# Two sister kernels' RG-LRU and norm edits joined in a two-block transformer, with MLA, dilated and neighbourhood reorderings

## The chip, the cores and the metric

The kernel runs on one core of a Trainium2 chip. The metric is the device time of one execution in microseconds, 3506.21 as the median of three runs (3505.55 to 3506.93). TensorE multiplies, VectorE, ScalarE and GpSimd do the elementwise work, SyncE issues the transfers. In the profile they are PE, DVE, ACT, POOL and SP, and PEld is TensorE's loading of stationary operands.

## What is computed

All data is float32, one sequence of 512 tokens with 1024 channels. The first block has two layers with three mixers side by side, gated, an output projection and a SwiGLU. The second has retention, a SwiGLU, an RG-LRU and a SwiGLU, each between two norms.

```python
def first_block(x, ...):
    for l in range(DEPTH):                                   # 2
        h = rms_norm(x, g_mix[l])
        c_q, c_kv, k_r, qkv_b, qkv_c, gate_logits = jnp.split(h @ w_in[l], IN_SPLITS, axis=-1)
        y_a = mla_mixer(c_q, c_kv, k_r, ...)                 # 8 heads, 512 x 512 scores
        y_b = dilated_mixer(q_b, k_b, v_b)                   # 3 patterns, banded
        y_c = neighbourhood_mixer(q_c, k_c, v_c, rpb[l])     # 8 heads, windows on a grid
        gates = jax.nn.sigmoid(gate_logits)
        x = x + (gates[0] * (y_a @ w_pa[l]) + gates[1] * (y_b @ w_pb[l]) + gates[2] * (y_c @ w_pc[l])) @ w_o[l]
        h = rms_norm(x, g_ffn[l])
        x = x + (jax.nn.silu(h @ w1[l]) * (h @ w3[l])) @ w2[l]
    return rms_norm(x, g_final)

def rglru_mixer(x, ...):
    y_branch, u = jnp.split(x @ w_in, 2, axis=-1)            # 1536 channels each
    y_branch = jax.nn.gelu(y_branch, approximate=True)
    u = conv4(u) + conv_b                                    # causal, per channel
    r, i = jax.nn.sigmoid(blocked(u, gate_w) + gate_b)       # 6 blocks of 256
    log_a = -8.0 * r * jax.nn.softplus(-a_param)
    a, mult = jnp.exp(log_a), jnp.sqrt(-jnp.expm1(2.0 * log_a))
    h = scan(a, mult * i * u)                                # h[t] = a[t] * h[t-1] + b[t]
    return (h * y_branch) @ w_out

def second_block(x, ...):
    for layer in range(DEPTH):
        m = retention_mixer(rms_norm(x), ...) if layer == 0 else rglru_mixer(rms_norm(x), ...)
        x = x + rms_norm(m, norm_g[layer, 1])
        x = x + rms_norm(swiglu_ffn(rms_norm(x, norm_g[layer, 2]), ...), norm_g[layer, 3])
```

## The kernel before

Activations lie with channels on the partitions and the 512 tokens along the free axis. Each float32 product is three TensorE passes: an operand is split into a high part and the rest (names in h and l: `zh` and `zl`, `u_ush` and `u_usl`, `u_hyh` and `u_hyl`), and high x high, low x high and high x low are added in a PSUM bank. Weights come in chunks of eight 128 x 128 tiles: SP's queue brings `raw`, ScalarE copies `wh` (line 525), VectorE subtracts `wl` (line 552), with a ring of three. The order of each engine is written by hand, one function for an engine and a stage (`tensor_`, `scalar_`, `vector_`, `gpsimd_`), and each engine runs in order. `wait_ge` is a wait on an event that another engine's `tell` announces; `claim(b, ...)` makes TensorE wait until the former contents of PSUM bank b have been read. The splits of the next chunks stand in ScalarE's and VectorE's programs where `ahead` or `reach(mark, n)` puts them: `reach` splits up to the n-th chunk behind a mark.

MLA (`tensor_mla`) runs 32 units of scores, with the transposes of probabilities `m_p` (by `ident`) three units later and the values, into bank 7, six later. Between the units TensorE takes tiles of the dilated projections from `rest`, eight to a group in bank 0, which ScalarE's `scalar_b` copies to `b_qk`, and query tiles from `q`. `scalar_y_move` and `vector_y_add` empty the values' bank into `m_yf`.

The dilated stage (`scalar_dil`, `vector_dil`) and the neighbourhood (`tensor_nbr`, `scalar_nbr`, `vector_nbr`, `gpsimd_nbr`) are iterations of the same kind. In the latter one iteration has two score tiles of 128 x 256; GpSimd divides `c_p` by its sum, and TensorE transposes the tiles of the iteration before.

A norm stage (`tensor_post`, named `ret`, `f20`, `f21`, `lru` in the tables `POST_BANK`, `POST_AT`) runs the last output tile `m7` in two halves of 256 tokens, takes the mean square by one-column matmuls with `ones`, spreads the root over the partitions (`hrows`), adds the result to `x`, and makes `z` for the next projection. For that projection's norm a tree (`TREE`) adds the eight squares `mb` on GpSimd and VectorE, and four one-column matmuls sum the rest (`tensor_next_stat`).

RG-LRU (`tensor_lru`, `scalar_lru`, `vector_lru`, `gpsimd_lru`) runs six blocks b of two channel tiles. TensorE: `gates(b)`, then the `u` and `y` projections of block b + 2, and the output's first pairs behind block 4. VectorE: scan of b - 1, conv of the next tiles in four steps (`vector_conv`, `u_uc`), their low part, `y_in` (which empties the y banks into `u_y`), low part of `hy`, then the recurrence: `vector_recur_in` (`iu`, and the relu `t`), `vector_recur` (`d`, `w`, `aa`). ScalarE does tanh, exp, square root and gelu's tanh, GpSimd the `+1` on `u_t`, gelu's products on `u_q` and the products with `u_g`. One buffer of a tile, `G[2]`, holds `t`, then the scan, then `hv`, until `hy` is read.

## Time and profile before

| what | us |
|---|---|
| median of 3 runs | 3506.21 |
| profiled execution | 3503.95 |
| its span | 3502.2 |
| TensorE busy | 3375.8 |
| VectorE busy | 1833.2 |
| ScalarE busy | 1285.5 |
| GpSimd busy | 626.8 |
| stretches: MLA of layer 0 / neighbourhood of layer 0 | 93.5 / 124.0 |
| norm after retention / after the first SwiGLU / after RG-LRU | 42.2 / 38.8 / 42.0 |
| RG-LRU | 265.6 |

The mean granted clock of TensorE is 0.983 of full speed. The rows further down are read so: a stretch's length beside the busy time of an engine tells how much of it the engine stood; a granted clock under 1.00 tells that part of the stretch ran at the lower of two levels (1.2 instead of 2.4 GHz); a wait is listed with the engine and tile that ended it.

### The profile page before, as it was taken

Reading aid. Unit: us, or ns where it says so; the run is one execution under the profiler, and the core shown is the slowest. Engines: PE = TensorE matmul, PEld = TensorE weight load, DVE = VectorE, ACT = ScalarE, POOL = GpSimd, SP = SyncE. Lnnn points to the kernel's source line nnn. Section 1 sums busy time; section 2 is a strip of 40 time slices with the busy share of each in tenths; the row PEclk is TensorE's granted clock in tenths of the full one; section 3 lists DMA queues with packets and bytes.
Section 4 is the critical chain, followed back from the end, with each engine's and each line's share of the span. In section 5 each row is a group of like instructions: output and inputs, shape, how many; then the busy total and the mean of one; then the engine's idle time right before and its main releaser. Section 6 shows DMA issues by size and latency. Waiting matters only on the chain.

```text
span 3502.2 us, 38259 instructions
## 1 busy us (share of the span) xinstructions
PE 3375.8 (96%) x15476; PEld 2788.2 (80%) x15476; DVE 1833.2 (52%) x2720; ACT 1285.5 (37%) x1958; POOL 626.8 (18%) x572
## 2 busy tenths in 40 slices
PE   8899999999999999999999999999999988889998
PEld 7787778888888877778888878888888876678887
DVE  6755565544437564655444455544444359855433
ACT  4643453322226433543332323333232235533221
POOL 1420122011003210221110022112110025431101
PEclk9999999999999999999999999999999999889999
DMA  3012223222221121223223222221323222222322
GB/s 131 31 61 73 74 89 99 97 96 98 99 93 55 49 73 64 89 83 102 91 96 105 98 75 82 88 90 67 102 97 97 84 67 76 75 72 97 96 96 85
DMA packets 85425, 296.91 MB, mean 85 GB/s; under 512 B 9472, under 2 KB 11776, under 8 KB 85248
## 3 DMA queue, kind: packets, MB, share of 16 engines
q1 hardware_dynamic: 85248, 294.47, 25.2%
q8 instruction: 122, 2.00, 0.2%
q14 instruction: 55, 0.45, 0.0%
HBM read 292.33 MB, written 2.10 MB: 84 GB/s over the span
## 4 chain that ended last, share of the span: by engine, by line
PE 83%; DVE 8%; ACT 4%; POOL 2%; issue 2%; DMA 0%; SPq 0%; POOLq 0%; DVEq 0%; ACTq 0%
PE bank L308 81%; PE bank L311 2%; DVE wl L552 2%; ACT wh L525 1%; POOL x L572 1%; DVE u_t L548 1%; POOL mb L572 1%; DVE u_uc L548 1%; DVE small L1198 1%; ACT c_k L525 1%; ACT u_g L528 0%; DVE u_t L545 0%; DVE m_ptl L552 0%; ACT b_v L525 0%; DVE c_kf L542 0%
## 5 line engine op out<-in xcount | busy, mean ns | idle before, releaser
L552 DVE TENSOR_TENSOR wl<-raw,wh 128x1024 fp32r<-128x1024 f32 (+1 forms) x532 | 681.1, 1283 | 902.6 <-ACT wh L525 899.7
L308 PE MATMUL bank<-zh,wh 128*128 128x512 f32 (+1 forms) x2668 | 1044.3, 391 | 20.6 <-ACT zh L525 7.8
L308 PE MATMUL bank<-zh,wl 128*128 128x512 f32 (+1 forms) x2668 | 1035.6, 388 | 14.3 <-DVE wl L552 14.3
L308 PE MATMUL bank<-zl,wh 128*128 128x512 f32 (+1 forms) x2668 | 1035.0, 388 | 14.2 <-DVE zl L555 14.0
L525 ACT ACTIVATE wh<-raw 128x1024 fp32r<-128x1024 f32 (+1 forms) x532 | 557.8, 1052 | 600.5 <-PE bank L308 499.9
L308 PEld LDWEIGHTS bank<-zh,wh 128*128 128x128 f32 x2668 | 509.4, 191 | 126.0 <-ACT zh L525 7.8
L308 PEld LDWEIGHTS bank<-zh,wl 128*128 128x128 f32 x2668 | 509.3, 191 | 122.0 <-DVE wl L552 20.2
L308 PEld LDWEIGHTS bank<-zl,wh 128*128 128x128 f32 x2668 | 509.3, 191 | 111.5 <-DVE zl L555 16.4
L308 PE MATMUL bank<-f_mh,wh 128*128 128x512 f32 (+1 forms) x748 | 285.0, 381 | 0.0
L308 PE MATMUL bank<-f_mh,wl 128*128 128x512 f32 (+1 forms) x748 | 283.0, 378 | 0.0
L308 PE MATMUL bank<-f_ml,wh 128*128 128x512 f32 (+1 forms) x748 | 282.1, 377 | 0.0
L572 POOL TENSOR_TENSOR f_t<-f_t 128x512 f32<-128x512 f32 x88 | 113.4, 1289 | 791.6 <-DVE f_t L548 791.6
L578 POOL TENSOR_TENSOR small<-small 128x1 f32<-128x1 f32 (+3 forms) x35 | 45.0, 1285 | 961.1 <-DVE small L545 961.1
L308 PEld LDWEIGHTS bank<-f_mh,wl 128*128 128x128 f32 x748 | 140.5, 188 | 28.9 <-DVE wl L552 0.4
L308 PE MATMUL bank<-wh,zh 128*128 128x512 f32 (+1 forms) x384 | 154.0, 401 | 8.7 <-ACT wh L525 4.1
L308 PEld LDWEIGHTS bank<-f_ml,wh 128*128 128x128 f32 x748 | 140.6, 188 | 26.8
L308 PEld LDWEIGHTS bank<-f_mh,wh 128*128 128x128 f32 x748 | 140.9, 188 | 25.6
L528 ACT ACTIVATE f_t<-f_t 128x512 f32<-128x512 f32 x88 | 55.6, 632 | 270.1 <-DVE f_t L542 270.0
L308 PE MATMUL bank<-wl,zh 128*128 128x512 f32 (+1 forms) x384 | 152.8, 398 | 0.5 <-DVE wl L552 0.5
L308 PE MATMUL bank<-wh,zl 128*128 128x512 f32 (+1 forms) x384 | 152.4, 397 | 0.0
L525 ACT ACTIVATE f_mh<-f_t 128x512 fp32r<-128x512 f32 x88 | 55.6, 632 | 227.2 <-POOL f_t L572 227.2
L542 DVE TENSOR_TENSOR f_t<-bank,rrow 128x512 f32<-128x512 f32 x88 | 60.7, 689 | 121.3 <-PE bank L308 110.7
(340 smaller groups left out, 4645.4 us busy)
## 6 DMA issues: line engine op xcount, KB each, us to landing
raw<-in_wts SPq DMA_DIRECT2D x530, 512.0 KB, 3.3
c_nb<-in_c_bias SPq DMA_DIRECT2D x16, 384.0 KB, 3.2
x<-in_xT SPq DMA_DIRECT2D x8, 256.0 KB, 6.6
out<-x SPq DMA_DIRECT2D x16, 128.0 KB, 1.9
b_mask<-in_b_mask SPq DMA_DIRECT2D x2, 576.0 KB, 3.7
r_d<-in_decay SPq DMA_DIRECT2D x4, 256.0 KB, 2.7
raw<-in_wts SPq DMA_DIRECT2D x2, 256.0 KB, 3.5
m_t<-in_mla_tab SPq DMA_DIRECT2D x2, 256.0 KB, 4.9
```

Source lines behind the costliest of these rows:

```text
L308: return self.e.matmul(out, l, r, start=start, stop=stop, skip_group_check=inside)
L311: return self.e.transpose(out, in_, self.m.ident)
L525: return self.e.activation(out, in_, ACT.Copy, scale=scale)
L528: return self.e.activation(out, in_, func, **kw)
L542: return self.e.tensor_tensor(out, a, b, op)
L548: return self.e.scalar_tensor_tensor(out, a, s, b, op0, op1)
L552: return self.e.tensor_tensor(out, src, b32(hi), ALU.subtract)
L572: return self.e.tensor_tensor(out, a, b, op)
L578: return self.e.tensor_tensor(out, v, self.m.negh[:, 0:n], ALU.pow)
L1198: L.e.tensor_reduce(m.mn[:, c:c + 1], m.bank[4 + i % 2], AX.X, ALU.min).then_inc(*L.tell("mn", "mla", l, i))
```

## The change

RG-LRU: conv step 0, relu, `+1`, `aa` and gelu's square term (times a constant, plus another) become ScalarE activations; the scan writes its own buffers `u_h`; the factor -0.125 moves from `hy` into the norm (`POST_SCALE`); the loops of ScalarE and VectorE and the splits among them (`LRU_REACH`) are put in another order; the tail's output pairs are cut into other chunks. Norms: the tree goes, and TensorE sums each square on its own, after each k of the second half's pass and in the next group. MLA: the values alternate between banks 1 and 7 (the last in 4), and the fill tiles are spread by a table over eight units. Neighbourhood: transposes, division and values move by one iteration. Dilated: the fill slots, and where the copy stands.

```diff
--- before.py
+++ after.py
...
+def values_bank(key, h):
+
+    if key[0] != "mla":
+        return 7
+    return {6: 7, 7: 4}.get(h, (1, 7)[h % 2])
...
-V_BANK = (4, 5, 0, 1)
+V_BANK = (5, 0, 1, 3)
...
-        next(rest, None)
+        for _ in range((0, 1, 1, 1, 2, 1, 1, 1)[i % 8] if i else 1):
+            next(rest, None)
...
-SLOTS = {0: [5] * 8 + [4] * 2, 1: [8] * 2 + [7] * 8}
+SLOTS = {0: [6] + [5] * 7 + [4, 3], 1: [8] * 2 + [7] * 8}
...
+        for n in () if p else at(p, i, 1):
+            scalar_b(L, ("b", l, 1) + n)
...
-    for it in range(18):
-        if 1 <= it < 17:
-            ps = L.claim(6, "lo", "pt", *key, it - 1)
-            for u in (2 * it - 2, 2 * it - 1):
+    for it in range(19):
+        if 2 <= it < 18:
+            j = it - 2
+            ps = L.claim(6, "lo", "pt", *key, j)
...
-        if it >= 3 and it % 2:
-            h = (it - 3) // 2
+        if it >= 4 and it % 2 == 0:
+            h = (it - 4) // 2
...
-            j = it - 1
+    for it in range(21):
+        if it >= 5 and it % 2 and it < 20:
+            scalar_y_move(L, m.b_yt, (it - 5) // 2, *key)
+        if 2 <= it < 18:
+            j = it - 2
...
         if 1 <= it < 17:
-            j = it - 1
+            for i in (2 * it - 2, 2 * it - 1):
+                vector_div(L, i, *key)
...
+POST_SCALE = {"ret": 1.0, "f20": 1.0, "f21": 1.0, "lru": -0.125}
+POST_AT = {"ret": 0, "f20": 3, "f21": 3, "lru": 0}
+POST_ROWS = {"ret": 7, "f20": 9, "f21": 9, "lru": 7}
...
-             [[("ev", "m7", s, h)] for h in range(2)], {(1, 2): squares, (1, 6): rows}, False)
+             [[("ev", "m7", s, h)] for h in range(2)], {(1, 2): squares, (1, POST_ROWS[s]): rows}, False)
...
-            if h == 0 and n == POST_AT[s]:
+            if h == 0 and n == POST_AT[s] + 1:
                 vector_m7(L, s, g, 1)
-            if h == 0 and n == max(POST_AT[s] + 1, 3):
+            if h == 0 and n == POST_AT[s] + 2:
+                if nxt:
+                    L.reach(("z2", s), 1)
                 stat(1)
-            if h or n > 1:
+            if nxt and h == 0 and n == POST_AT[s] + 4:
+                L.reach(("z2", s), 2)
+            if h:
...
-        for n, d in TREE[3:]:
-            L.wait_ge(*tree_ready(s, n, d, 1)[0])
-            L.wait_ge(*tree_ready(s, n, d, 1)[1])
-            L.tt(half(m.mb[n], 1), half(m.mb[n], 1), half(m.mb[n - d], 1), ALU.add).then_inc(
-                *L.tell("sq", "tree", s, n, d, 1))
...
-    def squares():
-        ps = L.claim(6, "rv", *N)
-        L.wait_ge("pl", "tree", s, 7, 4, 0)
-        L.wait_ge("sq", "tree", s, 7, 4, 1)
-        L.sums(ps, False, 0, m.mb[7], True).then_inc(*L.tell("st", "stat", *N))
-
-    return squares, L.spread(N)
+    def squares(h, ns):
+        def go():
+            ps = L.claim(6, "rv", *N) if (h, ns[0]) == (0, 0) else m.bank[6]
+            for n in ns:
+                L.wait_ge("cp", "xsq", s, n, h)
+                for r in (2 * h, 2 * h + 1):
+                    new = (h, n, r) == (0, 0, 0)
+                    t = L.mm(ps[:, r:r + 1], m.mb[n][:, 128 * r:128 * r + 128], m.ones, new, new or n == 7, not new)
+            if (h, ns[-1]) == (1, 7):
+                t.then_inc(*L.tell("st", "stat", *N))
+        return go
+
+    return ({(1, k): squares(0, (k,)) for k in range(8)}, {k: squares(1, (2 * k, 2 * k + 1)) for k in range(4)}, L.spread(N))
...
-             {(0, 1): squares1, (0, 3): rows1})
-    squares, rows = tensor_next_stat(L, prev)
+             {(0, 0): squares1, (0, 3): rows1, **early})
...
-            tensor_post_pair(L, "lru", 0, LW, x, lru_out_desc, range(8))
-    for i in (2, 4):
-        tensor_post_pair(L, "lru", i, LW, x, lru_out_desc, range(8))
+            for i in (0, 2):
+                tensor_post_pair(L, "lru", i, LW, x, lru_out_desc, range(8))
+    tensor_post_pair(L, "lru", 4, LW, x, lru_out_desc, range(8))
+    tensor_post_pair(L, "lru", 6, LW, x, lru_out_desc, range(10))
     for i in (0, 2, 4):
-        tensor_post_pair(L, "lru", i, LW, x, lru_out_desc, range(8, LW))
-    tensor_post(L, "lru", LW, x, lru_out_desc, 6)
+        tensor_post_pair(L, "lru", i, LW, x, lru_out_desc, range(8, 10))
+    for i in (0, 2, 4, 6):
+        tensor_post_pair(L, "lru", i, LW, x, lru_out_desc, range(10, LW))
+    tensor_post(L, "lru", LW, x, lru_out_desc, 8)
...
+def scalar_conv(L, n):
+
+    m = L.m
+    L.wait_ge("ev", "u", n)
+    if n > 3:
+        L.wait_ge("ev", "iu", n - 4)
+        L.wait_ge("lo", "us", n - 4)
+    L.fn(m.u_uc[n % 4], m.u_pad[n % 2][:, 0:512], ACT.Identity, scale=m.col("conv0")[:, n:n + 1],
+         bias=m.col("conv_b")[:, n:n + 1]).then_inc(*L.tell("cp", "conv", n))
...
+    L.wait_ge("cp", "y2", n)
+    L.fn(q, q, ACT.Identity, scale=0.044715 * 0.7978845608028654, bias=m.gel).then_inc(*L.tell("cp", "y3", n))
...
-            L.wait_ge("lo", "hy", j - 2)
+            L.wait_ge("ev", "d", j - 2)
+            L.wait_ge("th", "s", j - 2)
         L.fn(G[2], G[0], ACT.Tanh, scale=C, bias=C).then_inc(*L.tell("th", "t", j))
     for i in range(2):
         j = 2 * b + i
         G, C = recur_bufs(m, b, i), m.sp4[:, j:j + 1]
+        if b:
+            L.wait_ge("pl", "k", j - 2)
+            L.wait_ge("cp", "aa", j - 2)
         L.fn(G[3], G[0], ACT.Exp, scale=C, bias=C).then_inc(*L.tell("ex", "x", j))
+    for i in range(2):
+        j = 2 * b + i
+        G = recur_bufs(m, b, i)
+        L.wait_ge("th", "t", j)
+        L.fn(G[2], G[2], ACT.Relu).then_inc(*L.tell("cp", "t", j))
+        L.wait_ge("ex", "x", j)
+        L.fn(G[3], G[3], ACT.Identity, bias=m.ones).then_inc(*L.tell("cp", "v", j))
...
-        L.ts(G[2], G[2], 0.0, 1.0, ALU.max, ALU.mult).then_inc(*L.tell("ev", "t", j))
...
+def scalar_recur_a(L, b):
+    for i in range(2):
+        j = 2 * b + i
+        G = recur_bufs(L.m, b, i)
         L.wait_ge("ev", "w", j)
-        L.ts(G[4], G[3], -0.5, -1.0, ALU.mult, ALU.add).then_inc(*L.tell("ev", "aa", j))
+        L.fn(G[4], G[3], ACT.Identity, scale=-0.5, bias=L.m.neg1).then_inc(*L.tell("cp", "aa", j))
...
-        L.e.tensor_tensor_scan(G[2], G[4], G[0], 0.0, ALU.mult, ALU.add).then_inc(*L.tell("ev", "scan", j))
+        L.e.tensor_tensor_scan(L.m.u_h[i], G[4], G[0], 0.0, ALU.mult, ALU.add).then_inc(*L.tell("ev", "scan", j))
...
-LRU_REACH = {b: (2, 2, 3, 3, 4, 4) if b == 4 else (2, 3, 3, 4, 5, 6) for b in range(6)}
+LRU_REACH = (3, 3, 4, 5, 5, 6)
...
         lru_reach(L, b, 0)
-        for n in nxt:
-            scalar_us(L, n)
+        if b < 6:
+            scalar_recur(L, b)
         lru_reach(L, b, 1)
         if b:
             scalar_hy(L, b - 1)
+        for n in nxt:
+            scalar_us(L, n)
         lru_reach(L, b, 2)
-        if b < 6:
-            scalar_recur(L, b)
-        lru_reach(L, b, 3)
         for n in nxt:
             scalar_y_square(L, n)
+        lru_reach(L, b, 3)
         if b < 6:
             scalar_recur_sqrt(L, b)
+            scalar_recur_a(L, b)
...
         lru_reach(L, b, 0)
         if nxt:
             vector_conv(L, nxt)
+        lru_reach(L, b, 1)
+        if b:
+            vector_hy(L, b - 1)
         for n in nxt:
             vector_us(L, n)
-        lru_reach(L, b, 1)
         for n in nxt:
             vector_y_in(L, n)
-        if b:
-            vector_hy(L, b - 1)
+        if b < 6:
+            vector_recur_in(L, b)
         lru_reach(L, b, 2)
         if b < 6:
-            vector_recur_in(L, b)
+            vector_recur(L, b)
         lru_reach(L, b, 3)
-        if b < 6:
-            vector_recur(L, b)
-        lru_reach(L, b, 4)
         if b < 4:
             for n in (2 * b + 4, 2 * b + 5):
                 vector_pad(L, n)
+        lru_reach(L, b, 4)
         for n in nxt:
             vector_gelu(L, n)
...
```

VectorE in RG-LRU, from the scan of one block to the next; `u_t` is the recurrence, `u_uc` the conv, `u_g` the gates. Before:

```order
L3052 SCALAR_TENSOR_TENSOR u_t<-u_t,u_g 128x512 x2
L552 TENSOR_TENSOR wl<-raw,wh 128x1024
L545 TENSOR_SCALAR u_uc<-u_pad,cols 128x512 x2
L548 SCALAR_TENSOR_TENSOR u_uc<-u_pad,cols,u_uc 128x512 x6
L552 TENSOR_TENSOR u_usl<-u_uc,u_ush 128x512 x2
L552 TENSOR_TENSOR wl<-raw,wh 128x1024
L542 TENSOR_TENSOR u_y<-bank,rrow 128x512 x2
L555 SCALAR_TENSOR_TENSOR u_hyl<-u_t,u_hyh 128x512 x2
L548 SCALAR_TENSOR_TENSOR u_g<-u_g,u_uc 128x512 x2
L545 TENSOR_SCALAR u_t<-u_t 128x512 x2
```

After:

```order
L3076 SCALAR_TENSOR_TENSOR u_h<-u_t,u_g 128x512 x2
L553 TENSOR_TENSOR wl<-raw,wh 128x1024 x2
L549 SCALAR_TENSOR_TENSOR u_uc<-u_pad,cols,u_uc 128x512 x6
L553 TENSOR_TENSOR u_hyl<-u_h,u_hyh 128x512 x2
L553 TENSOR_TENSOR u_usl<-u_uc,u_ush 128x512 x2
L543 TENSOR_TENSOR u_y<-bank,rrow 128x512 x2
L549 SCALAR_TENSOR_TENSOR u_g<-u_g,u_uc 128x512 x2
L553 TENSOR_TENSOR wl<-raw,wh 128x1024
L549 SCALAR_TENSOR_TENSOR u_t<-u_t 128x512 x4
L553 TENSOR_TENSOR wl<-raw,wh 128x1024
L543 TENSOR_TENSOR u_pad<-bank,rrow 128x512 x2
```

The tensor-scalar steps are gone, `u_hyl` stands ahead of `u_usl` and `u_y`, two chunks are split behind the scan, and the last split before the recurrence `u_t` ... x4 is as it was.

ScalarE in the same block, from the gates' tanh (`u_g<-bank`) to the splits behind. Before:

```order
L528 ACTIVATE u_g<-bank,cols 128x512 x4
L525 ACTIVATE wh<-raw 128x1024
L525 ACTIVATE u_ush<-u_uc 128x512 x2
L525 ACTIVATE wh<-raw 128x1024
L525 ACTIVATE u_hyh<-u_t 128x512 x2
L528 ACTIVATE u_t<-u_g,cols 128x512 x2
L528 ACTIVATE u_t<-u_g,small 128x512 x2
L525 ACTIVATE wh<-raw 128x1024
L528 ACTIVATE u_q<-u_y 128x512 x2
L528 ACT_TABLE_LOAD
L528 ACTIVATE u_g<-u_t 128x512 x2
L525 ACTIVATE wh<-raw 128x1024
```

After:

```order
L529 ACTIVATE u_uc<-u_pad,cols 128x512 x2
L529 ACTIVATE u_g<-bank,cols 128x512 x4
L526 ACTIVATE wh<-raw 128x1024 x2
L529 ACTIVATE u_t<-u_g,cols 128x512 x2
L529 ACTIVATE u_t<-u_g,small 128x512 x2
L529 ACTIVATE u_t<-u_t 128x512
L529 ACTIVATE u_t<-u_t,small 128x512
L529 ACTIVATE u_t<-u_t 128x512
L529 ACTIVATE u_t<-u_t,small 128x512
L526 ACTIVATE u_hyh<-u_h 128x512 x2
L526 ACTIVATE u_ush<-u_uc 128x512 x2
L526 ACTIVATE wh<-raw 128x1024
```

The recurrence, with four further steps, now stands ahead of `u_hyh` and `u_ush`, and the conv's first step ahead of the gates.

TensorE in MLA's units 7 and 8 (`m_pth`, `m_ptl` with `m_v` are values, `zh`, `zl` with `wh1`, `wl1` fill tiles of bank 0, `m_zqh0` queries). Before:

```order
L308 MATMUL bank7<-m_ptl1,m_v 128x256
L308 MATMUL bank7<-m_pth1,m_v 128x256
L308 MATMUL bank7<-m_ptl1,m_v 128x256
L308 MATMUL bank0<-zh,wh1 128x512 [waits cp]
L308 MATMUL bank0<-zl,wh1 128x512
L308 MATMUL bank0<-zh,wl1 128x512
L311 MATMUL bank6<-ident,m_p2 128x128 [waits sc,lo]
L311 MATMUL bank6<-ident,m_p2 128x128 x3
L308 MATMUL bank5<-m_kah,m_qh0 128x512 [waits ex]
L308 MATMUL bank5<-m_kal,m_qh0 128x512
L308 MATMUL bank5<-m_kah,m_ql0 128x512
```

After:

```order
L309 MATMUL bank5<-m_kbh,m_qh1 128x512 [waits ex]
L309 MATMUL bank5<-m_kbl,m_qh1 128x512
L309 MATMUL bank5<-m_kbh,m_ql1 128x512
L309 MATMUL bank2<-m_zqh0,wh1 128x512 [waits ev]
L309 MATMUL bank2<-m_zql0,wh1 128x512
L309 MATMUL bank2<-m_zqh0,wl1 128x512
L309 MATMUL bank0<-zh,wh1 128x512 [waits cp]
L309 MATMUL bank0<-zl,wh1 128x512
L309 MATMUL bank0<-zh,wl1 128x512
L312 MATMUL bank3<-ident,m_p1 128x128 [waits sc,lo]
L312 MATMUL bank3<-ident,m_p1 128x128 x3
```

The fill tile that opens a new group, the one that waits for `cp`, stands behind the queries of unit 7 instead of the values of unit 8.

## Rows read from the trace of the kernel before

**Rows 1.** The page, part 1: busy us (share of span) xinstructions by engine
```profile
PE 3375.8 (96%) x15476; PEld 2788.2 (80%) x15476; DVE 1833.2 (52%) x2720; ACT 1285.5 (37%) x1958; POOL 626.8 (18%) x572
```

**Rows 2.** By stretch: length, busy PE PEld DVE ACT POOL, clock, DMA share, GB/s
```profile
414.00:538.00 124.00, 117.25 (x531) 90.70 (x530) 84.36 (x176) 63.96 (x129) 31.90 (x45) 0.97 0.24 79
2420.10:2462.30 42.20, 31.95 (x188) 29.23 (x187) 23.32 (x43) 16.78 (x34) 21.94 (x25) 0.80 0.16 51
2803.00:2841.80 38.80, 31.61 (x187) 29.15 (x186) 23.31 (x44) 15.84 (x32) 20.34 (x24) 0.82 0.21 69
3107.40:3149.40 42.00, 31.48 (x187) 29.04 (x187) 24.07 (x44) 17.59 (x36) 22.66 (x26) 0.80 0.15 51
```

**Rows 3.** Waits of TensorE, whole run: total us, times, longest
```profile
PE bank L308 <- DVE wl L552: 36.4, 17, 4.7
PE bank L308 <- DVE m_yf L542: 10.2, 8, 1.7
PE bank L311 <- POOL c_p L575: 8.9, 9, 2.0
PE bank L308 <- ACT b_qk L525: 6.4, 4, 1.9
PE bank L311 <- POOL b_p L575: 1.7, 2, 0.9
```

**Rows 4.** By stretch, RG-LRU: blocks one and three, and the tail
```profile
2878.20:2909.70 31.50, 27.91 (x122) 22.38 (x121) 29.47 (x33) 17.61 (x24) 13.90 (x11) 1.00 0.23 73
2946.60:2982.00 35.40, 30.06 (x123) 23.73 (x122) 30.44 (x35) 18.95 (x27) 15.88 (x13) 0.95 0.24 75
3018.00:3107.40 89.40, 79.87 (x359) 65.62 (x357) 67.38 (x74) 40.14 (x56) 29.37 (x22) 0.92 0.23 77
```

**Rows 5.** By tile, VectorE, 2878.2 to 3018: ns min/median/max, first, last start
```profile
L545 DVE TENSOR_SCALAR u_t<-u_t x16: 415/1161/1517, 2892.0 to 3006.2; 128x512 f32<-128x512 f32 x16
L552 DVE TENSOR_TENSOR wl<-raw,wh x20: 1214/1226/2309, 2879.9 to 3012.2; 128x1024 fp32r<-128x1024 f32 x20
L545 DVE TENSOR_SCALAR u_uc<-u_pad,cols x8: 535/543/543, 2881.1 to 2985.0; 128x512 f32<-128x512 f32 x8
```

**Rows 6.** Timeline, VectorE, third block: start, us, operation
```profile
2972.52 2.28 DVE L552 TENSOR_TENSOR wl<-raw,wh 128x1024 fp32r<-128x1024 f32 x1
```

**Rows 7.** Timeline, TensorE, same place; in brackets idle before and releaser
```profile
2974.85 0.80 PE L308 MATMUL bank<-u_ush,wl 128*128 128x512 f32 x1 [4.71 <-DVE wl L552]
```

**Rows 8.** Groups by shape, ScalarE, 2878.2 to 3018: busy us, mean ns, idle
```profile
L528 ACT ACTIVATE u_t<-u_g,cols 128x512 f32<-128x512 f32 x8 | 6.1, 807 | 6.3 <-DVE u_hyl L555 6.3
L528 ACT ACTIVATE u_q<-u_y 128x512 f32<-128x512 f32 x8 | 4.5, 614 | 0.0
```

**Rows 9.** Groups by shape, GpSimd, 2878.2 to 3018: busy us, mean ns, idle
```profile
L575 POOL TENSOR_SCALAR u_q<-u_q 128x512 f32<-128x512 f32 x8 | 8.5, 1069 | 3.4 <-ACT u_q L528 3.1
```

**Rows 10.** Waits of TensorE, 2419.5 to 2462.3, norm after retention
```profile
PE bank L308 <- DVE zl L555: 6.3, 3, 3.0
PE bank L308 <- DVE wl L552: 3.9, 1, 3.9
```

**Rows 11.** Timeline, TensorE: column sums, and the matmul behind them
```profile
2459.91 0.95 PE L308 MATMUL bank<-small,mb 128*128 128x1 f32 x8
2460.72 0.48 PE L308 MATMUL bank<-zh,wh 128*128 128x512 f32 x1
```

**Rows 12.** By tile, GpSimd, 2420 to 2465: ns min/median/max, first, last start
```profile
L572 POOL TENSOR_TENSOR mb<-mb x10: 722/771/924, 2443.4 to 2450.9; 128x256 f32<-128x256 f32 x10
```

**Rows 13.** Timeline, TensorE, MLA of the first layer, behind unit 7's queries
```profile
95.26 0.40 PE L308 MATMUL bank<-zh,wh 128*128 128x512 f32 x1
95.49 0.39 PE L308 MATMUL bank<-zl,wh 128*128 128x512 f32 x1
```

**Rows 14.** Timeline, ScalarE, same place: exp of unit 7, the copy
```profile
95.47 0.69 ACT L528 ACTIVATE m_p<-bank,small 128x512 f32<-128x512 f32 x1
96.16 0.60 ACT L525 ACTIVATE b_qk<-bank 128x512 f32<-128x512 f32 x1
```

More of the change, by code:

```diff
@@ L296, in block2 @@
         self.u_q = [T(f"u_q{i}", 52.25 + i) for i in range(2)]
+        self.u_h = [T(f"u_h{i}", 54.25 + i) for i in range(2)]
 class Pe(Line):
@@ L1161, in scalar_mla @@
     L.lead = 0
-    for i in range(40):
+    for i in range(41):
         if i and i % 8 == 0 and i <= 32:
@@ L1223, in gpsimd_mla @@
     m = L.m
-    for i in range(40):
+    for i in range(41):
         if 1 <= i < 33:
@@ L1489, in scalar_dil @@
             scalar_exp(L, i, m.b_p[i % 2], m.b_p[i % 2], *key)
+        for n in at(p, i, 1) if p else ():
+            if n[0] == "g":
+                scalar_gate(L, l, 0, n[1])
         if i in (5, 9):
@@ L1544, in vector_dil @@
                 *L.tell("mn", *key, i, 1))
+        for x, n in at(p, i, 1) if p else ():
+            if x == "g":
+                vector_gate(L, l, 0, n)
+            else:
+                vector_proj(L, l, 0, n)
         if 1 <= i < 9:
@@ L1774, in vector_nbr @@
     L.lead = 0
-    for it in range(20):
+    for it in range(21):
         if it < 16:
@@ L1805, in vector_nbr @@
                 (vector_gate if x == "g" else vector_proj)(L, l, 1, n)
+        if it >= 8 and it % 4 == 0:
+            vector_y(L, m.b_yf, *m.yc, (it - 8) // 4, (it - 8) // 4, *key)
+        for x, n in at_n(it, 2):
+            if x in "qk":
+                (vector_c_q_lo if x == "q" else vector_c_k_lo)(L, l, n)
         L.ahead()
@@ L1819, in gpsimd_nbr @@
     gpsimd_bias(L, l, 1)
-    for it in range(20):
-        if it < 16:
-            for i in (2 * it, 2 * it + 1):
+    for it in range(21):
+        if 1 <= it < 17:
+            for i in (2 * it - 2, 2 * it - 1):
                 gpsimd_div(L, i, L.m.c_p[i % 6], *key)
@@ L2598, in scalar_m7 @@
     L.wait_ge("mm", "acc", "m", s, 7, h)
-    L.fn(half(m.rrow, h), half(m.bank[POST_BANK[s][7 + h]], h), ACT.Square).then_inc(*L.tell("cp", "m7", s, h))
+    L.fn(half(m.rrow, h), half(m.bank[POST_BANK[s][7 + h]], h), ACT.Square,
+         scale=POST_SCALE[s]).then_inc(*L.tell("cp", "m7", s, h))
 def vector_m7(L, s, g, h):
@@ L2624, in scalar_post @@
             L.wait_ge("sq", "m", s, n - 1)
-        L.fn(m.sqt if n else m.sqa, m.bank[POST_BANK[s][n]], ACT.Square).then_inc(*L.tell("cp", "msq", s, n))
+        L.fn(m.sqt if n else m.sqa, m.bank[POST_BANK[s][n]], ACT.Square, scale=POST_SCALE[s]).then_inc(
+            *L.tell("cp", "msq", s, n))
     scalar_m7(L, s, 0)
@@ L2772, in tensor_ffn2 @@
         L.group(n, 8, L.z_whole(), f2_in_desc, [f_bank(i, w) for w in range(2)], [("ev",) + x for x in n],
-                {2: rows} if i == 2 else {})
+                {1: rows} if i == 2 else {})
     x = mids_of(L, F)
@@ L3097, in scalar_lru @@
     scalar_rows(L, ("z2", "f20"), False)
+    for n in range(2):
+        scalar_conv(L, n)
     for n in range(2):
@@ L3107, in scalar_lru @@
         nxt = (2 * b + 2, 2 * b + 3) if b < 5 else ()
+        for n in nxt:
+            scalar_conv(L, n)
         if b < 6:
```

154 lines of the change are left out of this document (56 added, 98 removed).

## The prediction

> **What bounds the kernel now.** I read the page first: TensorE is busy for 3375.8 of 3502.2 us [rows 1]. So there are two ways to gain, an idle TensorE and a TensorE at the lower clock, and the next views look for both. The table by stretch gives the places: the three output-norm stages (42.2, 38.8 and 42.0 us) and the neighbourhood (124.0 us) are places in which TensorE is neither full nor at clock 1.00 [rows 2], and so are the RG-LRU's blocks and tail [rows 4]. The list of TensorE's waits names the causes over the whole run: 36.4 us for a low weight half (`wl`), 10.2 us for the MLA values' bank (`m_yf`), 8.9 us for neighbourhood probabilities (`c_p`), 6.4 us for `b_qk`, 1.7 us for `b_p` [rows 3]. All of them stand on VectorE, ScalarE or GpSimd, in-order engines that had something else ahead.
>
> Every sum is made against the profiled execution, 3503.95 us; the median shown, 3506.21, lies 2.26 us above, and I add that at the end. About 0.2% (7 us) is what a measurement of this kernel can tell from no change.
>
> **RG-LRU, the four blocks between gates 0 and gates 4.** They take 2878.2 to 3018.0, 139.8 us, 31.5 for the first and 35.4 for the third [rows 4]. TensorE needs 27.9 us for a block, its busy time in the first, at clock 1.00 [rows 4]. VectorE sets the pace: two tensor-scalar steps on each `u_t` (relu and `aa`, 16 in four blocks) take 415 to 1517 ns, the low weight half 1214 ns, but up to 2309 [rows 5]. In the third block one takes 2.28 us, and starts behind those [rows 6]; TensorE stands 4.71 us for it and then falls to the lower clock, which the block's 0.95 holds [rows 4, 7].
>
> The change takes from VectorE, per block, 2 conv steps of 0.54, 2 relus of at least 0.42 and 2 `aa` of up to 1.52: 4 us or so of 30.4 [rows 4, 5]. GpSimd loses two `+1` and two gelu steps of 1.07 [rows 9]. ScalarE gains ten operations: two with two pointers of 0.81, the others like the square of 0.61: 2 x 0.81 + 8 x 0.61 = 6.5 us, on an engine that the third block keeps waiting (18.95 busy of 35.4) [rows 4, 8]. The new order puts `wl` ahead of `y_in`, and the scan writes a buffer of its own, so that the tanh of the next block no longer waits for `hy`.
>
> What is late next? `y_in` now stands behind `hy` and `us`, and these stand behind ScalarE's longer recurrence: TensorE's next y pair claims the bank that `y_in` empties. From a walk through the new order with these durations I find TensorE stopped there about 1.5 us a block, which gives 29.4; a stretched operation more or less makes it 28.2 to 31.0. I take 29.6, since the wait adds up behind in-order engines: 4 x 29.6 = 118.4, **-21 us** (-16 to -27).
>
> A rule speaks against this part. The Trainium skill (Perfetto Trace Analysis, "Optimizing Scalar/DVE Operations") says that an operation for which VectorE has a fast mode is quicker there and that moving it pays if VectorE is saturated. By the page's average it isn't (52%), and the six steps would cost ScalarE more than they free; the sum by that would be 0 for this term. In this stretch VectorE is busy 30.44 of 35.40 us, so I take the stage.
>
> **RG-LRU, start and tail.** The start (conv 0 on ScalarE, rows of `z` earlier) gives **-2** (0 to -4). From gates 4 to the end of the output's sixth pair it is 89.4 us with TensorE busy 79.9 at clock 0.92 [rows 4]: 9.5 us idle and, at 8% of the clock, 7.2 lost. The new order puts four output chunks ahead of gates 5, which covers most of that idle time, not the wait for the last `hy`: **-10** (-5 to -15).
>
> **Output norms (three stages, 123.0 us).** Their clock is 0.80 to 0.82 [rows 2]. In the first TensorE waits 6.3 us for `zl` and 3.9 for `wl` [rows 10]. The latter is held by the adds of the tree, ten of 722 to 924 ns on GpSimd and four on VectorE, which VectorE's split of the next chunk stands behind [rows 12]; the tree goes. In its place TensorE sums the columns: eight one-column matmuls are 0.81 us for four of the program's [rows 11], 28 more a stage are 5.7 us, 17.0 in all. Eight of them a stage stand in the second pass, where TensorE waits for `zl` anyway; the later ones have no cover. So: gaps and clock loss over the three stages are 28 idle and 24 of clock (20% of 42.2, 18% of 38.8, 20% of 42.0); 17 comes on; what goes is 11 of `wl` wait, the clock loss behind it (some 8), and some 9 of `zl` from sums and splits that come earlier. -28 + 17 = **-11** (+6 if only the `wl` wait goes, -19).
>
> **Neighbourhood (twice).** The transposes wait for GpSimd's division of the same iteration, 8.9 us over both layers [rows 3], and the clock of 0.97 over 124 us is 3.7 more [rows 2]. One iteration later the division is done. Next is `c_kl`, whose low half VectorE makes after the gates now; I leave about 1.5 us a layer: **-8** (-3 to -12).
>
> **MLA (twice).** Two banks for the values take off most of the 10.2 us for `m_yf`, but where it waits 1.7 the chain of `q` on VectorE is next, so I count 5, and 3 of `b_qk` and of the first values. Against that stands a wait the change adds: fill tiles move within the eight units, and the ninth, 17th and 25th open a new group in bank 0 one unit earlier, before ScalarE has copied the old. In the profile TensorE is behind the queries of unit 7 at 95.26 and goes on with the eighth tile; after the change the ninth stands there. ScalarE's exp of unit 7 starts at 95.47 and the copy that it would wait for comes behind it, 96.16 + 0.60 [rows 13, 14]. That is 1.5 us, six times: +9. Queued behind it on TensorE are the transposes and the scores of the next unit. Net **+1** (-6 to +7).
>
> **Dilated and tail.** Of `b_p` (1.7) and what is left of `b_qk` I count **-3** (0 to -5) [rows 3]. In the last norm the rows come nine 256-column matmuls later, at half the 0.23 us between two 512-column ones [rows 13] about 1 us, with cover for half: **+0.5** (0 to +1).
>
> Sum: -21 - 2 - 10 - 11 - 8 + 1 - 3 + 0.5 = **-53.5**: 3450.5 profiled, **3452.7** median.
>
> **Rivals.** (a) More goes than I count. If VectorE's and GpSimd's operations stretch each other (0.415 against 1.517, 1.214 against 2.309 [rows 5]) and six fewer a block ends it, the blocks come to 28, the tail to 75, and the norm stages to 104: -28 - 3 - 15 - 19 with -11 for the neighbourhood, -5 for the dilated stage and -3 for MLA is -84, or 3422. The Trainium skill (SBUF — State Buffer, "Who interferes with whom") has it as a lock: the later of the two waits the other out, and ScalarE never waits; the rows' stretch of about 1.1 us is what it would look like. For it: the steps' median of 1.161 us lies nearer the long end. Against: the scan, conv and GpSimd's large adds stay. (b) The sums on TensorE aren't covered: norm stages +6 instead of -11, 3470. For it: the last half of the sums stands in a group with nothing to wait for. (c) The recurrence on ScalarE makes a longer chain, blocks at 32.5 (130 in all, -10), tail -4, the others near their weak bounds (norms -8, neighbourhood -5, MLA +3, dilated -2): -26, 3480; with blocks at 38 (152, +12) it is -4, no difference. (d) Slower: ScalarE as the new limit. `aa` now stands behind the square root, which loads a table, and the scan, `hv`, `hy`, `us` and `y_in` stand behind `aa`, in this order on two engines. If each handover is late the loop slips by a chain, not by an engine. The other terms are -20.5 without the LRU; five blocks have to rise by over 4.1 us, from 35.0 to 39.1, for the kernel to be slower. At 42: 5 x 7 - 20.5 = +14.5, 3521. Against it: ScalarE's 18.95 + 6.5 is 25.5 of 35.4. That the change doesn't do what it says is out for the moved instructions, which stand in the new order; a wait that only moves to the next event is in (c).
>
> **How the numbers follow.** The forecast has 0.44 (3438 to 3465), (a) 0.16, (b) 0.13, (c) 0.18, of which 0.05 are within 0.2%, (d) 0.09. Faster by over 0.2%: 0.44 + 0.16 + 0.13 + 0.13 = 0.86; same 0.05; slower 0.09. The range goes from 3422, (a), to 3490, (c) without its part close to zero; 0.18 lie outside.
>
> **What would show it.** LRU blocks of 29 to 30 us between gates, no `wl` wait over 1 us there, and waits for `u_y` of 1 to 2 us. In the norms no `wl` wait of 3 to 4 us, one-column matmuls of 0.2 us each, and stages of 37 to 40. In MLA waits for `b_qk` of about 1.5 us three times a layer, none for `m_yf` over 1. In the neighbourhood no `c_p` wait over 0.5. I am wrong if a block takes over 32 us, or if the norm stages don't shrink.

## The result, and the profile after

The changed kernel takes 3467.82 us (median of four runs, 3462.23 to 3471.03) against 3505.99, the kernel before measured alongside, a ratio of 0.9889 with a 95% interval of 0.9872 to 0.9906: 38 us faster. The forecast was 3452.7, with a range of 3422 to 3490. The size is 15 us short: two terms of the sum are wrong by 20 us together, in the same direction, and others came out a little better.

The span went from 3502.2 to 3466.1 us. The table sets the stages of the two traces side by side, each from the end of one named group of matmuls to the end of another. The first row runs from the last tile of MLA's value projection to the neighbourhood's first score group, in both layers; MLA's own row ends a little inside the dilated stage, so it is longer than the 93.5 us a layer of the table ahead.

| stage | before | after | change | forecast |
|---|---|---|---|---|
| MLA and dilated, twice | 676.4 | 689.7 | +13.3 | -2 |
| of these MLA | 270.8 | 284.8 | +14.0 | +1 |
| neighbourhood, twice | 256.0 | 255.0 | -1.0 | -8 |
| three norm stages | 123.0 | 111.4 | -11.7 | -11 |
| RG-LRU, start to gates 0 | 36.4 | 33.9 | -2.6 | -2 |
| gates 0 to gates 4 | 139.7 | 115.1 | -24.7 | -21 |
| RG-LRU's tail | 89.4 | 81.0 | -8.4 | -10 |
| all else | | | -1.0 | +0.5 |

The page of the changed kernel (busy us, share of the span, instructions) has the answer to [rows 1]. TensorE is busy as long as before, in a span 36 us shorter:

```profile
PE 3376.0 (97%) x15644; PEld 2796.1 (81%) x15644; DVE 1796.0 (52%) x2674; ACT 1321.6 (38%) x2018; POOL 600.6 (17%) x518
```

TensorE's waits in the changed kernel, whole run (total us, times, longest), beside [rows 3]:

```profile
PE bank L309 <- ACT b_qk L526: 16.2, 8, 3.1
PE bank L309 <- DVE c_kl L553: 10.4, 4, 3.8
...
PE bank L309 <- DVE m_kal L553: 8.0, 4, 2.3
...
PE bank L309 <- DVE u_y L543: 4.9, 3, 1.8
...
PE bank L309 <- DVE wl L553: 1.2, 2, 0.7
...
PE bank L309 <- DVE m_yf L543: 0.9, 2, 0.6
```

Of 36.4 us for `wl` 1.2 are left, of 10.2 for `m_yf` 0.9, and `c_p` is gone. But `b_qk` rose from 6.4 to 16.2, and two names are new with more than a few us: `c_kl` (0.9 before) and `m_kal`. That is where most of the missing time is: beside the forecast 13 us are missing in MLA, 7 in the neighbourhood and 2 in the dilated stage.

The stretches of the changed kernel (length, busy PE PEld DVE ACT POOL, clock, DMA) that answer to [rows 2, 4], the norms first, then RG-LRU's second and fourth block and its tail:

```profile
2432.67:2470.46 37.79, 33.30 (x243) 31.70 (x243) 21.02 (x39) 17.37 (x36) 13.83 (x15) 0.95 0.18 60
2810.96:2847.77 36.81, 34.56 (x244) 33.30 (x244) 19.64 (x36) 16.21 (x33) 11.82 (x13) 0.91 0.23 75
...
2908.90:2937.90 29.00, 27.71 (x122) 22.52 (x121) 26.26 (x29) 24.99 (x37) 17.16 (x8) 1.00 0.29 99
...
2967.30:2996.70 29.40, 27.62 (x121) 22.42 (x120) 27.30 (x30) 24.98 (x36) 18.50 (x8) 1.00 0.26 90
2996.70:3077.70 81.00, 76.67 (x359) 64.31 (x358) 59.00 (x67) 48.36 (x70) 35.37 (x18) 0.96 0.26 87
3077.70:3114.50 36.80, 34.31 (x244) 32.61 (x243) 21.07 (x39) 17.36 (x36) 13.86 (x15) 0.91 0.19 61
```

A block takes 29.4 us with TensorE busy 27.6 at full clock, where the third took 35.4 at 0.95. The norms have a clock of 0.91 to 0.95 instead of 0.80 to 0.82.

Now the new waits, each with what stands in front. In MLA, TensorE (timeline; start, us, in brackets idle before and what ended it) behind the queries of unit 7, and ScalarE in front of that, the place of [rows 13, 14]:

```profile
98.53 0.50 PE L309 MATMUL bank<-zh,wh 128*128 128x512 f32 x1 [2.33 <-ACT b_qk L526]
```

```profile
96.27 0.69 ACT L529 ACTIVATE m_p<-bank,small 128x512 f32<-128x512 f32 x1 [0.65 <-DVE small L1209]
...
96.94 1.04 ACT L526 ACTIVATE wh<-raw 128x1024 fp32r<-128x1024 f32 x1
97.89 0.58 ACT L526 ACTIVATE b_qk<-bank 128x512 f32<-128x512 f32 x1
```

The wait forecast is there, at the forecast place, behind exp of unit 7. A weight split of 1.04 us stands between exp and copy as well. This is so at the first of the six forecast waits only. Four of them are 1.3 to 1.5 us, and in the longest, 3.15 us in the first layer, no split stands there: exp itself starts late, since the maximum that it waits for stands behind a split on VectorE. TensorE, ScalarE and VectorE there:

```profile
152.56 0.79 PE L309 MATMUL bank<-zh,wh 128*128 128x512 f32 x1 [3.15 <-ACT b_qk L526]
```

```profile
151.25 0.69 ACT L529 ACTIVATE m_p<-bank,small 128x512 f32<-128x512 f32 x1 [1.66 <-DVE small L1209]
```

```profile
149.14 1.47 DVE L553 TENSOR_TENSOR wl<-raw,wh 128x1024 fp32r<-128x1024 f32 x1 [1.65 <-ACT wh L526]
```

Some 20 us after the first of these waits, TensorE stands before values in bank 1, and VectorE (below it) has been making the low part of keys from that same bank, behind the addition that empties the values' other bank:

```profile
118.97 0.39 PE L309 MATMUL bank<-m_pth,m_v 128*128 128x256 f32 x1 [1.75 <-DVE m_kal L553]
```

```profile
116.81 0.67 DVE L553 TENSOR_TENSOR m_ptl<-bank,m_pth 128x512 fp32r<-128x512 f32 x1
117.52 0.68 DVE L543 TENSOR_TENSOR m_yf<-bank,m_yt 64x512 f32<-64x512 f32 x1
118.23 0.68 DVE L553 TENSOR_TENSOR m_kal<-bank,m_kah 64x512 fp32r<-64x512 f32 x1
```

The neighbourhood, TensorE before scores of the third head pair, and VectorE ahead of it:

```profile
473.94 0.58 PE L309 MATMUL bank<-c_k,c_q 128*128 128x256 f32 x1 [3.78 <-DVE c_kl L553]
```

```profile
469.22 0.68 DVE L543 TENSOR_TENSOR f_g<-bank,rrow 128x512 f32<-128x512 f32 x1
470.66 0.69 DVE L549 SCALAR_TENSOR_TENSOR f_g<-f_g,bank 128x512 f32<-128x512 f32 x1 [0.77 <-ACT f_g L529]
471.27 2.62 DVE L553 TENSOR_TENSOR c_kl<-c_kf,c_k 64x640 fp32r<-64x640 f32 x2
```

The low keys stand behind a gate and its projection, which itself waited 0.77 us for ScalarE.

### The profile page after: what moved, and what is told of

Read it like the earlier page. It is cut to its first block, busy times and chain, and to the rows that moved or that the text cites. A ratio compares the mean times of both kernels' runs of the same rounds, so it can differ in the third digit from the quotient of the medians.

```text
span 3466.1 us, 38536 instructions
## 1 busy us (share of the span) xinstructions
PE 3376.0 (97%) x15644; PEld 2796.1 (81%) x15644; DVE 1796.0 (52%) x2674; ACT 1321.6 (38%) x2018; POOL 600.6 (17%) x518
## 3 DMA queue, kind: packets, MB, share of 16 engines
q1 hardware_dynamic: 85248, 294.47, 25.5%
## 4 chain that ended last, share of the span: by engine, by line
PE 89%; DVE 6%; ACT 3%; issue 1%; POOL 1%; DMA 0%; SPq 0%; POOLq 0%; DVEq 0%; ACTq 0%
PE bank L309 87%; PE bank L312 2%; DVE wl L553 1%; ACT wh L526 1%; DVE small L1209 1%; DVE u_uc L549 1%; DVE m_ptl L553 0%; ACT u_g L529 0%; ACT b_v L526 0%; ACT m_p L529 0%; ACT c_k L526 0%; POOL x L573 0%; DVE m_yf L543 0%; DVE c_kl L553 0%; POOL u_g L573 0%
## 5 line engine op out<-in xcount | busy, mean ns | idle before, releaser
L309 PE MATMUL bank<-zh,wh 128*128 128x512 f32 (+1 forms) x2668 | 1043.5, 391 | 30.0 <-ACT b_qk L526 11.1
L543 DVE TENSOR_TENSOR f_t<-bank,rrow 128x512 f32<-128x512 f32 x88 | 60.7, 689 | 123.3 <-PE bank L309 112.6
## 6 DMA issues: line engine op xcount, KB each, us to landing
x<-in_xT SPq DMA_DIRECT2D x8, 256.0 KB, 6.5
r_d<-in_decay SPq DMA_DIRECT2D x4, 256.0 KB, 2.7
raw<-in_wts SPq DMA_DIRECT2D x2, 256.0 KB, 3.4
m_t<-in_mla_tab SPq DMA_DIRECT2D x2, 256.0 KB, 4.9
```

Source lines behind the costliest of these rows:

```text
L309: return self.e.matmul(out, l, r, start=start, stop=stop, skip_group_check=inside)
L543: return self.e.tensor_tensor(out, a, b, op)
```

## Experiments

Each kernel is the changed kernel with the edit shown (the last two join edits); times are medians of four runs and compare with 3467.82. Stage lengths are taken as in the table, from one trace each. The kernel before was measured beside every group of runs, with medians of 3503.2 to 3506.0, so a difference of 2 or 3 us between kernels of different groups says nothing. Stages vary too, where the code of the stage is the same: MLA as changed takes 281.0 to 286.8 us in eight traces, the neighbourhood as changed 252.8 to 255.0 in nine (253.9 on the mean; the changed kernel's own is the longest), the three norm stages 109.5 to 112.4, RG-LRU 228.6 to 231.4.

**MLA.** Three kernels separate fill order and value banks. All of MLA back, which also splits the values one unit earlier again:

```diff
-V_BANK = (5, 0, 1, 3)
+V_BANK = (4, 5, 0, 1)
...
-    return {6: 7, 7: 4}.get(h, (1, 7)[h % 2])
+    return 7
...
-        for _ in range((0, 1, 1, 1, 2, 1, 1, 1)[i % 8] if i else 1):
-            next(rest, None)
+        next(rest, None)
```

> The changed kernel with MLA's value banks (all in bank 7), fill order (one tile a unit) and value split put back as they were before. Own theory: MLA as changed costs 16 us net (7 in the first layer, 9 in the second, by the ends of the stages in the two traces), nothing behind it depends on it, so this kernel is 16 us faster than the changed one, about 3452, with b_qk waits of 6 instead of 16 us and none for m_kal; m_yf waits of 10 come back. Rival A: the loss only stands in MLA because the dilated stage behind took it back (that stage gained 5.6 where 3 were expected), so 16 - 5 = 10 or less comes, about 3458. Rival B: what was lost in MLA is a clock or other accident of that run: no difference, 3468.

It took 3450.29 us (ratio to before 0.9843, 0.9828 to 0.9858), 17.5 less than the changed kernel. MLA is 270.3 us, where it was 270.8 before. So the loss is MLA's, and nothing behind it took it back. Only the fill order back (the last hunk above):

> The changed kernel with one fill tile after each unit, as before, but with the values in the two banks. Own theory: the b_qk waits at units 7, 15 and 23 (2.33, 1.39, 3.15 and 1.34, 1.52, 1.39 us) come from the fill tile that opens a group one unit early and go, about -9 to -11, 3458; the waits for m_kal (8.0 us, four times) belong to the values in bank 1, which the keys use too, and stay. Rival: VectorE's chain of the unit sets MLA's pace and the wait only shows up under another name: less than 4 us of difference, 3464 to 3468.

3453.97 us, 13.9 less and more than the 9 to 11 expected, and MLA 272.3. Its waits in MLA's first layer and the start of the dilated stage (total, times, longest):

```profile
PE bank L309 <- DVE m_kal L553: 5.3, 3, 2.4
PE bank L309 <- ACT b_qk L526: 1.4, 1, 1.4
PE bank L309 <- DVE m_yf L543: 1.3, 1, 1.3
```

The fill order cost 12.5 us of the 14. With one tile a unit, the two banks (with the values split a unit later) gain nothing over one: the time is 3.7 us longer than with all of MLA back, MLA 2.0, which is inside its variation. The `m_kal` waits are what `m_yf` was in the first kernel of this group, which has this in the same stretch:

```profile
PE bank L309 <- DVE m_yf L543: 5.7, 4, 1.7
PE bank L309 <- ACT b_qk L526: 3.5, 2, 1.9
```

Only the banks back (the first two hunks):

> The changed kernel with MLA's values all in bank 7 and the value banks as before, but with the changed fill order and the values' split one unit later. Own theory: the fill order costs 14 (what the run with one tile a unit gave back) and the two banks some 3.5, separately, so this gains 3.5: 3464. Rival: fill order and banks belong together, since the places without a fill tile are those of the values; with one bank the values' waits of 1.6 us come back on top: 3468 to 3475.

3469.24 us, MLA 286.6: no gain. With the fill order as changed the banks are worth nothing measurable, the waits for `m_yf` come in the place of those for `m_kal`, and `b_qk` still stands there, 9.6 us in the first layer:

```profile
PE bank L309 <- ACT b_qk L526: 9.6, 4, 3.8
PE bank L309 <- DVE m_yf L543: 4.1, 5, 1.3
```

My theory's 3464 was missed and the rival's 3468 to 3475 met, with the waits for the values back on top, as it said. Its reason, that the banks need the fill order, isn't shown: MLA is 1.8 us shorter with two banks in the changed order and 2.0 longer with one tile a unit, both inside its variation. The three kernels show the fill order as the cost, 12.5 us of MLA with two banks and 16.3 with one (286.6 against 270.3), and no clear gain from the banks.

**Neighbourhood.** The low parts ahead of the gates again:

```diff
+        for x, n in at_n(it, 2):
+            if x in "qk":
+                (vector_c_q_lo if x == "q" else vector_c_k_lo)(L, l, n)
         for x, n in at_n(it, 1):
             if x in "qk":
                 (vector_c_q if x == "q" else vector_c_k)(L, l, n)
...
-        for x, n in at_n(it, 2):
-            if x in "qk":
-                (vector_c_q_lo if x == "q" else vector_c_k_lo)(L, l, n)
```

> The changed kernel with one thing moved: in the neighbourhood's VectorE iteration the low parts of queries and keys stand ahead of the gate and its projection again, as before. Own theory: the c_kl waits of 3.78, 1.50, 3.77 and 1.38 us come from this order alone (lo of the keys stands behind a projection that waits for ScalarE's gate); they shrink to under 1 us each, the clock drops behind the long ones (6.8 us at half speed each) go, -8 to -12 in all, 3458. Rival: one iteration later everything else is late too, and the wait moves to the gate's bank or to the transposes: less than 3 us, 3465 to 3468.

3461.18 us, 6.6 less, short of the 8 to 12 expected; the two stages together are 250.4 instead of 255.0. Two more kernels with the same neighbourhood, the joined ones further down, have 252.2 and 252.1, so the stages gain 2 to 5 us. The time's own interval overlaps with the changed kernel's. TensorE's waits in the first, this kernel and then the changed one:

```profile
PE bank L312 <- DVE c_ptl L553: 2.4, 1, 2.4
PE bank L309 <- DVE c_kl L553: 1.6, 2, 0.9
```

```profile
PE bank L309 <- DVE c_kl L553: 5.3, 2, 3.8
...
PE bank L312 <- DVE c_ptl L553: 0.3, 1, 0.3
```

The order was the cause of the `c_kl` waits (10.4 us in both layers, 3.3 here); a part comes back as a wait for `c_ptl`, the low part of the transposed probabilities, which the low keys now precede. The whole stage back as before:

> The changed kernel with the neighbourhood as before (transposes one iteration after the scores, low parts of queries and keys ahead of the gates, its fill slots). Own theory: by the ends of the stages in the two traces the changed neighbourhood gains 0.6 and 0.4 us only, because c_kl waits of 3.8 and 1.5 us came in the place of those for c_p, so going back costs about 1: 3469. Rival (the prediction's term): it gains 8, and something else of the changed kernel loses; then 3476.

3473.40 us, 5.6 more, between the two figures, with intervals of some 6 us: the time doesn't settle it. By the traces the waits for `c_p` are back (8.9 us, as in [rows 3]), and the stages are 257.3, and 256.0 in the kernel before, against the 252.8 to 255.0 above. So the step as changed is worth 1 to 5 us in its stage, and not the 8 forecast.

**RG-LRU.** Two kernels undo one half each. The steps on their old engines, in the changed order (conv, gelu and `+1` likewise):

```diff
-        L.fn(G[2], G[2], ACT.Relu).then_inc(*L.tell("cp", "t", j))
+        L.ts(G[2], G[2], 0.0, 1.0, ALU.max, ALU.mult).then_inc(*L.tell("ev", "t", j))
...
-        L.fn(G[4], G[3], ACT.Identity, scale=-0.5, bias=L.m.neg1).then_inc(*L.tell("cp", "aa", j))
+        L.ts(G[4], G[3], -0.5, -1.0, ALU.mult, ALU.add).then_inc(*L.tell("ev", "aa", j))
```

> The changed kernel with RG-LRU's linear steps back on their old engines (conv step 0, relu and aa on VectorE, the +1 and gelu's square term on GpSimd), in the changed order and with the scan's own buffers. Own theory: VectorE's load set the pace of a block, and 4 us or more of it come back with their stretching, so blocks rise from 29.4 to about 33.5, five of them and the tail: +18 to +25, 3485 to 3493. Rival A: the order, with splits ahead of the recurrence and the freed buffer, gave the gain; then this kernel is within 5 us of the changed one, 3468 to 3473.

3488.10 us, 20.3 more. The order as before, steps on ScalarE (VectorE's and ScalarE's loop, as in the diff ahead, and this):

```diff
-LRU_REACH = (3, 3, 4, 5, 5, 6)
+LRU_REACH = {b: (2, 2, 3, 3, 4, 4) if b == 4 else (2, 3, 3, 4, 5, 6) for b in range(6)}
```

> The changed kernel with ScalarE's and VectorE's order in RG-LRU's loop, and the numbers of splits in it, as they were before; the linear steps stay on ScalarE, the scan keeps its own buffers. Own theory: the moved steps carry most of the gain, so blocks rise from 29.4 to 31 or 32, +8 to +12, 3476 to 3480. Rival A (order): wl waits of 3 to 5 us a block come back as before, +20 or more, 3488 and up. If this and the run with the steps put back each lose nearly all of the 35 us that RG-LRU gained, neither does it alone.

3485.80 us, 18 more, nearly twice what I expected and short of the rival. TensorE's waits in RG-LRU with the steps put back, and then with the order put back:

```profile
PE bank L309 <- DVE u_y L543: 12.4, 4, 5.4
...
PE bank L309 <- DVE wl L553: 3.0, 4, 1.7
```

```profile
PE bank L309 <- ACT wh L526: 10.5, 6, 3.3
PE bank L309 <- DVE wl L553: 7.2, 9, 1.6
```

RG-LRU takes 265.6 us before, 249.6 with the order alone, 250.4 with the steps alone, 229.9 with both. Alone they bring 16 and 15, together 35.7. Without the steps moved, VectorE gets to `y_in` late (`u_y`); without the order, the splits stand behind ScalarE's longer recurrence (`wh`): right in front of the late ones are the square root and the two `aa`. Neither does it alone, and my theory that the steps carry most of it falls. Both kernels keep the scan's own buffers and the tail's other chunks, so "alone" includes these, and no run here shows what they bring. The tail tells one thing of them: it takes 89.4 us before, 81.7 with the steps put back and 88.9 with the order put back, so its gain hangs on the order of ScalarE and VectorE, and with TensorE's new chunks but without that order it is only 0.5 shorter.

What was left, `u_y`, by moving `y_in` ahead of `hy` and `us`:

```diff
+        for n in nxt:
+            vector_y_in(L, n)
         if b:
             vector_hy(L, b - 1)
         for n in nxt:
             vector_us(L, n)
-        for n in nxt:
-            vector_y_in(L, n)
```

> The changed kernel with one thing moved: in VectorE's RG-LRU block y_in stands ahead of the low parts of hy and us. Own theory (the prediction's): the u_y waits of 1.29, 1.78 and 1.78 us come from y_in's place behind these four operations of 0.68; moved ahead they go, blocks fall by 1 to 2 us, -3 to -5 in all, 3464. Rival: the loop is set by the chain through hy and us, not by the bank: the same waits come back before the gates (u_usl) or hy, no difference or some us slower, 3467 to 3472.

3466.22 us, 1.6 less, inside the intervals. In RG-LRU the changed kernel waits for

```profile
PE bank L309 <- DVE u_y L543: 4.9, 3, 1.8
...
PE bank L309 <- DVE u_hyl L553: 2.0, 1, 2.0
```

and this one for

```profile
PE bank L309 <- DVE u_hyl L553: 5.4, 1, 5.4
...
PE bank L309 <- DVE u_y L543: 2.3, 2, 1.5
```

Gates 0 to 4 fall from 115.1 to 112.5, the tail rises from 81.0 to 85.0: `hy` of block 3 is late instead. The place of `y_in` is a part of the cause of `u_y` (2.3 of 4.9 us stay), and moving it is worth nothing, since the tail loses what the blocks gain.

**Norms.** The tree, the four sums, the splits and the second half's statistics back at their old places:

> The changed kernel with the norm stages and the sums for the next norm as before: tree of adds on GpSimd and VectorE, four column sums, splits and second half's statistics at their old places. Own theory: the three stages give back the 12 us that they gained by the ends of the stages in the two traces (4.7, 2.1 and 5.2), 3480, with wl waits of 3.5 to 3.9 us behind the tree and the low clock there. Rival: the gain is not the tree but the clock, which comes by what ran before; then 3 us or less, 3471.

3479.88 us, 12.1 more; the stages are 121.5 instead of 111.4, where they were 123.0 before. The first of them waits as in [rows 10]:

```profile
PE bank L309 <- DVE zl L556: 6.3, 3, 3.0
PE bank L309 <- DVE wl L553: 3.7, 1, 3.7
```

The price of the sums, by leaving some out (14 of the second half's 16 a stage):

```diff
-            for n in ns:
+            for n in ns if not h else ns[1:] if ns[1] == 7 else ():
```

> The changed kernel without 14 of the 16 column sums of the next norm's second half, in each of the three norm stages (the squares of seven of eight channel tiles are left out of the sums for tokens 256 to 511, so the scales there are wrong; nothing else is left out). It measures what TensorE pays for the sums that stand in the group behind the halves. Own theory: nothing covers them there, 42 at 0.2 us are 8.5 us, 3459. Rival: TensorE has slack in that group that waits take up, since the root and the rows behind it set the end; then 3 us or less, 3465 to 3468.

3458.48 us, 9.3 less; the three stages are 102.7, 8.7 less for 42 sums, 0.21 us each. The first, to be read beside its 37.79 above:

```profile
2429.69:2464.27 34.58, 30.09 (x215) 28.60 (x215) 20.99 (x39) 17.37 (x36) 13.82 (x15) 0.95 0.20 66
```

They stand uncovered, as the prediction had it.

**Versions that beat both.** MLA as before, the low parts first, `y_in` first in blocks 0 to 3, and at RG-LRU's start one chunk split earlier on ScalarE:

```diff
     for n in range(2):
         scalar_us(L, n)
         L.ahead()
+    L.reach(("lru", 0), -1)
     for n in range(2):
         scalar_y_square(L, n)
```

> A joined version: the changed kernel with MLA as before, with the neighbourhood's low parts ahead of the gates, with y_in ahead of hy and us in RG-LRU's blocks 0 to 3 (not in block 4, where hy waited 5.4 us behind it), and with the last chunk before gates 0 split ahead of the square and gelu's tanh at RG-LRU's start. Own theory: the parts add up: 3450.3 for MLA, -7 for the low parts, -3.9 for the waits of 3.36 and 0.53 us at the start, -3 for u_y: about 3436. Rival: the low clock and in-order engines take part of it back, 3445.

3442.79 us (ratio 0.9825, 0.9810 to 0.9839): 6 short of the sum of its parts. The stretch before gates 0 fell from 33.9 to 28.5. The `y_in` part gave nothing again: gates 0 to 4 and the tail take 112.6 and 83.5, together 196.1 as in the changed kernel. On top of it, splits ahead of retention's first turn and ahead of the norm's rows (on ScalarE and VectorE alike):

```diff
     for h in range(4):
+        if not h:
+            L.ahead()
         scalar_ret_qk(L, "rq", h)
...
     stat(0)
+    if nxt:
+        L.reach(("z2", s), 0)
     for h in range(2):
```

> The joined version with three splits earlier: in retention the first chunk ahead of the first query turn (TensorE waits 4.15 us for its wh there, in the kernel before too), and in the norm stages the first chunk of the next projection ahead of the rows (waits of 1.55 and 0.70 us behind the first SwiGLU). Own theory: these three waits go, -6 us, 3437. Rival: the split ahead of the turn delays the turn's own chain by 1 us of ScalarE and 1.2 of VectorE, which TensorE needs next: -3 or less, 3440 to 3443.

3436.32 us, ratio 0.9804 (0.9789 to 0.9820), the fastest here: 67 us below the kernel before in the same group (3503.68), and as my theory had it. The stretch from the second neighbourhood's end to the norm after retention is 4.6 us shorter than without these splits, and the norm stage after the first SwiGLU takes 33.9 instead of 36.8. Its longest waits are old ones:

```profile
PE bank L309 <- DVE m_yf L543: 10.2, 8, 1.7
PE bank L309 <- DVE zl L556: 9.0, 6, 2.1
PE bank L309 <- ACT zh L526: 8.0, 1, 8.0
PE bank L309 <- ACT b_qk L526: 5.4, 3, 1.9
```

## Why the prediction was right, and where it failed

**Right: RG-LRU's mechanism and size.** Blocks of 29.6 were forecast and 27.3, 29.0, 29.4 and 29.4 came; waits for `u_y` of 1.3 to 1.8 us stand where the walk put them. ScalarE is busy 25.0 us a block, against 25.5 worked out. VectorE being full in its stretch, not on the page's average, was the right reading: putting the steps back costs 20 us. The sum had no price for the order apart from the steps, and the runs show that undoing it costs nearly as much, 18 us. For the tail the number fits (-8.4 for -10), but not the reason: the new chunks ahead of gates 5 don't carry it without the order.

**Right: the norms.** -11 forecast, -11.7 measured, and both halves of it hold in runs of their own: the whole step is worth 10 to 12 net, and a sum costs 0.21 us where 0.20 was taken. What the tree brings apart from the splits that moved with it, no run shows.

**Failed: "but where it waits 1.7 the chain of q on VectorE is next, so I count 5".** I looked at what followed the `m_yf` wait on VectorE, not at who else used the second bank. Values in bank 1 wait for the low part of keys that are read from it, 8.0 us, and most of the 10.2 came back under another name: two banks bring no clear gain over one, with either fill order.

**Failed in size: "that is 1.5 us, six times: +9".** The mechanism and the place were right, and four of the six waits are 1.3 to 1.5 us. The other two, in the first layer, are 2.33 and 3.15, each behind a weight split, which makes 11.1 us of the six; the last group of the fill (2.1 and 3.0 us, 1.9 each before) is later too. The runs put the fill order at 12.5 us. With the gain of the banks that didn't come, that makes +14 out of +1, outside the term's own range.

**Failed: "Next is c_kl ... I leave about 1.5 us a layer".** The order was read rightly and its price too low: 5.3 us in the first layer and 5.1 in the second. The projection ahead of the low keys waits for ScalarE's gate, which I didn't count. Moving the two operations back gives 2 to 5 us in the stages; that the 8 forecast are there is not shown.

**Small terms.** The dilated stage was put at -3 and gave -0.7, within its range; the last norm and everything else gave -1.0 where +0.5 was put.

**Rivals.** (a) is out: the stretch didn't end (last section), and no block fell to the time of TensorE alone but the first. (b) is out as a sum, though its premise holds: the late sums are uncovered, and the stages gain more than they cost. That the time came within 2 us of its 3470, and 3 us outside the band of the forecast itself (3438 to 3465), is chance: the norms gained their 11.7, and MLA and the neighbourhood lost instead. (c) and (d) named ScalarE's chain; with the order undone TensorE waits for splits behind it, and two blocks take 32.2 and 33.6, near the 32.5 of (c). The new order is what avoids it.

**Signs.** Nearly all of them came: blocks, `u_y`, no long `wl`, the price of a sum, `b_qk`, no `m_yf` and no `c_p`. Two names that made the time miss, `m_kal` and `c_kl`, were not among them.
